# b_down added as a column on VectorE where it reads the transposed block from PSUM, zeros in DRAM in place of computed first sums, and the late modulation in f16 halves

## The reference, cut to what matters

```python
logits = h @ router_w + router_b
top_v, top_i = lax.top_k(logits, 4); gates = softmax(top_v)
gu  = xblk @ w_gu[e] + b_gu[e]                 # for the tokens of expert e
act = (clip(up) + 1.0) * gate * sigmoid(1.702 * gate)
yb  = act @ w_down[e] + b_down[e]
y   = sum over a token's four experts of yb * gate
x   = x + mod[:, 5] * rmsnorm(y, norm_g[3])
```

## Time and profile before

| | us |
|---|---|
| median of 3 runs | 2680.45 (2677.73 to 2681.34) |
| the profiled execution | 2680.32 |
| its span | 2678.6 |
| busy PE | 2439.7 (91%) |
| busy DVE | 1797.7 (67%) |
| busy ACT | 1553.6 (58%) |
| busy POOL | 799.2 (30%) |
| DMA | 536.90 MB, 200 GB/s over the span |

### The profile page before, as it was taken

One profiled execution on the slowest core, in us unless ns is written; L12 is line 12 of the kernel. 1 busy time (PEld: TensorE's weight loads), 2 busy tenths in 40 slices (PEclk: granted clock), 3 DMA queues, 4 the chain that ended last, 5 costly groups with the idle time before them and its releaser, 6 DMA issues. The chain is left out here.

```text
span 2678.6 us, 135745 instructions
## 1 busy us (share of the span) xinstructions
PE 2439.7 (91%) x57165; PEld 2162.2 (81%) x57165; DVE 1797.7 (67%) x2118; ACT 1553.6 (58%) x1964; POOL 799.2 (30%) x629
## 2 busy tenths in 40 slices
PE   6999998999989758999999999888998999999993
PEld 2555558999985448999898989888898999999993
DVE  3784986666657773361818386778777786789883
ACT  4523544555554442462827476777776676778773
POOL 3111105677740121221122222323222223232321
PEclk8899998999999968999999999999999999999996
DMA  8621001011023274381929496889888887899966
GB/s 286 248 76 56 1 1 49 25 31 31 23 70 101 95 291 138 119 308 29 356 73 331 125 370 225 305 312 376 320 304 310 311 299 256 281 337 359 344 238 207
DMA packets 123432, 536.90 MB, mean 200 GB/s; under 512 B 12237, under 2 KB 12609, under 8 KB 90561
## 3 DMA queue, kind: packets, MB, share of 16 engines
q1 hardware_dynamic: 107120, 481.80, 47.9%
q0 software_dynamic: 14880, 48.91, 8.2%
q10 hardware_dynamic: 1360, 5.24, 0.5%
HBM read 496.99 MB, written 38.92 MB: 200 GB/s over the span
## 5 line engine op out<-in xcount | busy, mean ns | idle before, releaser
L2499 PE MATMUL ps<-qkv,weights 128*128 128x64 f16 x10496 | 937.8, 193 | 65.9 <-DVE weights L1915 32.9
L2499 PEld LDWEIGHTS ps<-qkv,weights 128*128 128x128 f16 x10496 | 921.9, 98 | 82.4 <-issue 41.4
L2501 PE MATMUL ps<-qkv,weights 128*128 128x64 f16 x10496 | 937.4, 193 | 2.3 <-issue 2.3
L2500 PE MATMUL ps<-qkv,weights 128*128 128x64 f16 x10496 | 937.3, 193 | 0.5 <-issue 0.5
L2501 PEld LDWEIGHTS ps<-qkv,weights 128*128 128x128 f16 x10496 | 922.4, 98 | 0.6 <-issue 0.6
L2500 PEld LDWEIGHTS ps<-qkv,weights 128*128 128x128 f16 x10496 | 922.4, 98 | 0.0
L1915 DVE SCALAR_TENSOR_TENSOR weights<-hT,weights 128x2048 f16<-128x2048 f16 (+1 forms) x256 | 585.9, 2338 | 167.4 <-ACT weights L1299 137.4
L1299 ACT ACTIVATE weights<-hT 128x2048 f16 (+1 forms) x256 | 527.8, 2103 | 83.9 <-DMA hT<-in_w_gu_dram 67.0
L2516 PE MATMUL ps<-qkv,weights 128*128 128x64 f16 x5248 | 472.1, 193 | 23.4 <-DVE weights L1920 21.1
L2516 PEld LDWEIGHTS ps<-qkv,weights 128*128 128x128 f16 x5248 | 461.3, 98 | 30.8 <-DVE weights L1920 26.3
L2517 PE MATMUL ps<-qkv,weights 128*128 128x64 f16 x5248 | 471.8, 193 | 0.0
(11 more groups left out here) (446 smaller groups left out, 4305.0 us busy)
## 6 DMA issues: line engine op xcount, KB each, us to landing
hT<-in_w_gu_dram SPq DMA_DIRECT2D x256, 1024.0 KB, 9.1
qkv<-in_w_down_dram SPq DMA_DIRECT2D x128, 1024.0 KB, 6.1
weights<-in_w_ada_dram SPq DMA_DIRECT2D x8, 2048.0 KB, 14.1
qkv<-in_w_in_dram SPq DMA_DIRECT2D x4, 2048.0 KB, 9.2
qkv<-in_w_ada_dram SPq DMA_DIRECT2D x4, 2048.0 KB, 9.3
hT<-decay_rows SPq DMA_DIRECT2D x20, 256.0 KB, 3.3
hT<-beta_rows SPq DMA_DIRECT2D x20, 256.0 KB, 3.3
qkv<-in_x_dram ACTq DMA_DIRECT2D x4, 1024.0 KB, 8.1
```

Source lines behind the costliest of these rows:

```text
L2499: pe.matmul(dst, ghi[k][:, b, c], xT[:, 0, k, :], start=first, stop=False, skip_group_check=True)
L2500: pe.matmul(dst, ghi[k][:, b, c], xT[:, 1, k, :], start=False, stop=False, skip_group_check=True)
L2501: last = pe.matmul(dst, glo[k][:, b, c], xT[:, 0, k, :], start=False, stop=end, skip_group_check=True)
```

## The change: what it does

1. The first sums are gone: no `lgm`, `mixe3`, `y_start`, `copy_y_start`, `store_y_start`, nor the waits for them. b_down is loaded once rather than three times.
2. `y_scratch` is filled with zeros, by two DMAs of 2 MB on SP's queue during DeltaNet; the loads of decay and beta rows of the later chunks wait for them (`s_zero` 65 for 33).
3. PE turns b_down (32 x 1024) by eight transposes into columns, ACT copies them to `bdT`, 32 experts x 8 columns.
4. `copy_yT` goes from ACT to DVE. There it is one operation that reads PSUM, scales and adds the expert's eight columns, each repeated over 64 rows. It stands in DVE's iteration t behind `next_down(t+1)`.
5. Late modulation: DVE's sums get a factor (`csw` for `cs`), ACT makes f16 high halves of the eight sums (in the stage of the Z tiles), POOL the low halves, and PE sums each by two f16 matmuls against an f16 column of 1/WSCALE.

```diff
             for i in range(2):
+                sp.dma_start(y_d[i * SEQ // 2:(i + 1) * SEQ // 2, :].rearrange("(p r) d -> p (r d)", p=P),
+                             slot(5)).then_inc(s_zero, 16)
+            sp.wait_ge(s_zero, 65)
...
+            for q in range(FIRST, NADA):
+                pool.wait_ge(s_adar, q + 1)
+                high, low = (sum_halves[q - FIRST][:, j] for j in range(2))
+                pool.tensor_tensor(low, sums_of[q - FIRST], high, ALU.subtract).then_inc(s_colT, 1)
...
             gather(0)
-            for n in range(NT):
-                store_y_start(n)
             gather(1)
...
-            for i in range(2):
-                pool.wait_ge(s_yin[i], 16 * (5 - 2 * i))
...
+                for q in {0: range(FIRST, FIRST + 4), 3: (8,), 5: (9,), 6: (10,), 7: (11,)}.get(g - G_Z, ()):
+                    act.wait_ge(s_mod, q + 1)
...
+                    act.activation(sum_halves[q - FIRST][:, 0], sums_of[q - FIRST], ACT.Copy).then_inc(s_adar, 1)
...
-            def copy_yT(t):
-                act.wait_ge(s_dn, t * DK + 2 * DK)
-                reached(act, s_ty, t, 1, EMPTY)
-                act.activation(yT, ps[:, BT, :].rearrange("p (c t) -> p c t", c=8), ACT.Copy,
-                               scale=1.0 / (ALPHA * WSCALE * WSCALE)).then_inc(s_yT, 1)
...
                     high_act(t + 1)
-                    copy_yT(t)
                     scale_y(t - 1)
...
+            def copy_yT(t, e):
+                dve.wait_ge(s_dn, t * DK + 2 * DK)
+                reached(dve, s_ty, t, 1, EMPTY)
+                dve.scalar_tensor_tensor(yT, ps[:, BT, :].rearrange("p (c t) -> p c t", c=8), 1.0 / (ALPHA * WSCALE * WSCALE),
+                                         bdT[:, bass.ds(e * 8, 8)].unsqueeze(2).to_broadcast([P, 8, B]), ALU.mult,
+                                         ALU.add).then_inc(s_yT, 1)
...
                     next_down(t + 1, new1, r1)
+                    copy_yT(t, expert(t))
                     dve.sem_inc(s_idle, 1)
+            copy_yT(nlast, expert(nlast))
...
-                            last = pe.matmul(ps[:, 6, n:n + 1], sums_of[q - FIRST][:, a * P:(a + 1) * P], ones[:, 0:1],
-                                             start=True, stop=True)
+                            for j in range(2):
+                                last = pe.matmul(ps[:, 6, n:n + 1], sum_halves[q - FIRST][:, j, a * P:(a + 1) * P],
+                                                 ones16[:, 0:1], start=j == 0, stop=j == 1)
...
+            for k in range(KD):
+                last = pe.transpose(ps[:, 2, k * NE:(k + 1) * NE], bdn[:, k * P:(k + 1) * P], ident[0:NE, 0:NE])
+            last.then_inc(s_bdT, 1)
```

More of the change, by code:

```diff
@@ L148, in hybrid_block @@
         sums_of += [QK[:, 6 * D + 384 + 512 * i:6 * D + 896 + 512 * i] for i in range(1, 5)]
+        sum_halves = [QK[:, a:a + 512] for a in (14 * D, 14 * D + 512, 9 * D + 384, 5 * D + 384)] + sums_of[0:4]
+        sum_halves = [a.bitcast(F16).rearrange("p (j n) -> p j n", j=2) for a in sum_halves]
         tail = QK[:, 6 * D + 384:6 * D + 384 + 5 * 512]
@@ L157, in hybrid_block @@
         ident = sb("ident", [P, P])
-        ones = sb("ones", [P, P])
+        bdT = sb("ones_and_iota_then_b_down", [P, NE * KD])
+        ones, iota = bdT[:, 0:P], bdT[:, P:2 * P]
         tri = sb("tri", [P, DIRS, P])
@@ L251, in hybrid_block @@
         work = W[:, 12288:12288 + NT * TOPK * NE]
[L252 to L256, removed]
+        bdn = QK[0:NE, 14336:14336 + D]
         work = work.rearrange("p (n k e) -> p n k e", n=NT, k=TOPK)
@@ L617, in _ @@
                 load_rows(s, False)
-            sp.wait_ge(s_zero, 33)
+            for i in range(2):
+                sp.dma_start(y_d[i * SEQ // 2:(i + 1) * SEQ // 2, :].rearrange("(p r) d -> p (r d)", p=P),
+                             slot(5)).then_inc(s_zero, 16)
+            sp.wait_ge(s_zero, 65)
             with sp.Fori(NC, NA) as s:
@@ L625, in _ @@
             sp.dma_start(bgu_raw[0:NE, :], b_gu[0]).then_inc(s_bgu, 16)
-            for j in range(3):
-                sp.dma_start(bdn[j * NE:(j + 1) * NE, :], b_down[0]).then_inc(s_small, 16)
+            sp.dma_start(bdn, b_down[0]).then_inc(s_small, 16)
             sp.dma_start(rw, router_w[0].rearrange("(k p) e -> p k e", p=P)).then_inc(s_rw, 16)
@@ L1349, in scale_y @@
                                scale=gtab[:, bass.ds(t, 1)]).then_inc(s_yc, 1)
[L1351 to L1354, removed]
             def token_one_hots(q):
@@ L1366, in _ @@
             act.wait_ge(s_nb, 4)
[L1367 to L1374, removed]
+            for q in range(4):
+                token_one_hots(q)
+            act.wait_ge(s_bdT, 1)
+            act.activation(bdT[:].rearrange("p (e c) -> p c e", e=NE), ps[:, 2, 0:NE * KD].rearrange("p (c e) -> p c e", c=KD),
+                           ACT.Copy).then_inc(s_bdT, 1)
+            for k in range(4):
                 high_gate_up(0, 0, k)
-            copy_y_start(5)
-            high_gate_up(0, 0, 3)
-            copy_y_start(6)
             copy_xT(0)
             name_rows(1)
-            high_gate_up(0, 0, 4)
-            copy_y_start(7)
-            for k in range(5, GK):
+            for k in range(4, GK):
                 high_gate_up(0, 0, k)
-            for i in range(2):
-                act.wait_ge(s_yin[i], 16 * (5 - 2 * i))
             act.wait_ge(s_meta, 2)
-            act.sem_inc(s_yT, EMPTY)
             act.sem_inc(s_yc, EMPTY + 1)
@@ L1428, in _ @@
             scale_y(nprev)
-            copy_yT(nlast)
             scale_y(nlast)
@@ L1498, in weighted_rows @@
                 sums = sums_of[q - FIRST]
-                link(dve.tensor_scalar(sums, staged(q)[:, 0, :], cs[:, 0, 0:1], None, ALU.mult))
+                link(dve.tensor_scalar(sums, staged(q)[:, 0, :], csw[:, 0:1], None, ALU.mult))
                 for k in range(1, KD):
-                    link(dve.scalar_tensor_tensor(sums, staged(q)[:, k, :], cs[:, k, 0:1], sums, ALU.mult, ALU.add))
+                    link(dve.scalar_tensor_tensor(sums, staged(q)[:, k, :], csw[:, k:k + 1], sums, ALU.mult, ALU.add))
                 dve.sem_inc(s_mod, 1)
@@ L1991, in _ @@
             next_down(1, new, r)
+            copy_yT(0, expert(0))
             with dve.Fori(1, MAXB) as t:
@@ L2439, in _ @@
             pe.matmul(ps[0:1, 4, 256:256 + NB], endf[:], active, start=True, stop=True).then_inc(s_cnt, 1)
-            pe.wait_ge(s_mixe, 1)
+            pe.wait_ge(s_small, 146)
             pe.wait_ge(s_bgu, 19)
[L2443 to L2461, removed]
+            for k in range(KD):
+                last = pe.transpose(ps[:, 2, k * NE:(k + 1) * NE], bdn[:, k * P:(k + 1) * P], ident[0:NE, 0:NE])
+            last.then_inc(s_bdT, 1)
             M = NT * TOPK
             for m in range(M):
-                if m == 16:
-                    y_start(4)
                 if m % 8 == 0:
@@ L2527, in turn_y @@
                 last.then_inc(s_ty, 1)
-            pe.wait_ge(s_yev, 4)
+            pe.wait_ge(s_bdT, 2)
             turn_x(0)
-            y_start(6)
-            y_start(7)
             pe.sem_inc(s_dn, DK)
```

44 lines of the change are left out of this document (15 added, 29 removed).

## The result

The changed kernel takes 2718.69 us, median of 4 runs (2712.83 to 2724.20), beside 2679.09 for the kernel before (4 runs): ratio 1.0155, 95% interval 1.0132 to 1.0177. The forecast was 2714, slower. By the medians the change costs 39.6 us, where +34 was forecast. So some 7 us of the difference of the medians are in no trace.

What follows compares the result with a forecast made beforehand. PE (TensorE) was taken as the bound, other engines and DMA mattering only where PE waits. Terms -10.4 + 0 - 0.8 - 14 + 38 + 18 + 3 = +34 on 2680.3 gave 2714 us, range 2684 to 2730.

Steps and rivals of the forecast that it cites:

- part 1: Projections: 64 f16 passes replace 64 fp32 passes on PE and the clock holds; -10.4 us (-5.3 to -10.5).
- part 2: Zeros to y_scratch on SP's queue: written before the later row loads matter; 0 us (0 to +4).
- part 3: Output and router stage: small DVE operations and ACT copies go, most of them beside PE; -0.8 us (0 to -3).
- part 4: Start of expert loop: without the stores, DVE's idle time before L1915 and the gather wait go; -14 us (-9 to -20).
- part 5: Expert loop: copy_yT behind four low down chunks on DVE makes PE wait at nine places; +38 us (25 to 50).
- part 5b: Same nine places: PE's clock falls to half behind the waits, 2.0 us a place; +18 us (0 to +30).
- elsewhere in the loop: Other blocks: DVE has one more 0.69 us operation per block, mostly in its waits for PE; +3 us (-3 to +7).
- The mark that was set for the clock: Expert loop, nine places: granted clock shows half; a row staying full in the loop's first half would make the forecast wrong.
- rival D: Loop start doesn't give its 14 us and the clock falls in the modulation anyhow: 2727 us; chance 0.10.
- Rival B: Nine places in the loop: the waits come but the clock holds: 2696 us; chance 0.15.
- rival C: Nine places: the delay is given back, as PE's later waits shrink by the same amount: 2658 us; chance 0.15.

Runs made afterwards that it cites:

- the run with the increments: Changed kernel plus 31 one-instruction increments of an idle semaphore on PE ahead of the expert loop: 2713.28 us, ratio 1.0141 to the kernel before.
- the copy by case: Changed kernel, copy_yT ahead of the low down chunks where the block after next has a new expert, else behind the first: 2687.73 us, ratio 0.9975, slower chip.

## Why the prediction was right, and where two of its terms weren't

| term | forecast | trace after |
|---|---|---|
| part 1, modulation | -10.4 | -10.2 (first tile behind it 240.81 to 230.65; the passes began 0.24 later) |
| part 2, zeros | 0 | +0.2 (the shift is 10.2 at the start of DeltaNet, 10.0 at its end) |
| part 3, router stage | -0.8 | -1.0 |
| part 4, start of the loop | -14 | -7.9 |
| part 5, nine waits | +38 | +37.3 |
| part 5b, half clock | +18 | +16.1 |
| elsewhere in the loop | +3 | -2.0 |
| sum | +34 | +32.5 |

The three lines above the sum, in the last column, come from the ledger: before turn_y +68.2, in turn_y -2.7, in down -12.1, together +53.4. Of that 16.1 is the half clock (all that turn_y and down take over their undisturbed length in the kernel after, 7.0 and 9.1, as no chase of chunks is left in them), 37.3 the waits.

That the sum is within 2 us of the trace is in part luck: part 4 is 6.1 too high a gain, the rest of the loop 5.0 too high a cost, and they nearly cancel. The mark that was set for the clock, its row in the first half of the loop, was too coarse to be one: it shows 9 in every slice from 1017 to 2643 us, as before, while the clock fell nine times. Read as it was written it would have spoken against a forecast that was right. And rival D's 2727 doesn't follow from its terms: 14 + 5 above 2714 is 2733, and half of that 2724.

**Part 1** came out as worked out, with the clock held. The bound with the fall was not needed: 64 passes in 1.74 us are 27 ns each. The Trainium skill (TensorE: Matmul & The Clock Gate, LDWEIGHTS) gives, by its formula, 107 ns for a load of 128 columns; the profile's record of a load in the loop does last 98 ns, but loads overlap, so it is no measure of the time from one to the next, and the measured 27 decides.

**Part 5** is the step on which the result hangs, and the order on DVE gave it right: the wait of 8.41 us for 8.5, at nine places, released by the copy. The experiments show it by one instruction's place.

**Part 5b** rests on the row at 1005.70 and on part 1's rows. The trace after has one fall of the clock at each of the nine places, 6.8 or 10.2 us long, and in the run with PE kept busy down has its full speed at seven of them. Rival B is out. The Trainium skill (TensorE: Matmul & The Clock Gate, HAM oscillation) describes such a fall in each wait, and this trace agrees.

**Part 4 was mis-sized** by 6 us. The step that failed is "what they can win is DVE's idle time before L1915": DVE's waits there did shrink, from 7.4 to 3.2 us (2.15 and 1.08), but gate_up(0) is as long as before. It could have been seen: in the trace before no wait of PE from 984 to 1016 names L1915, so DVE's idle time didn't end in one of PE's. What makes gate_up(0) long in both traces is holes without a releaser (2.3 us before, 2.9 after) and the clock at half, after for the first 3 us and again behind the hole. What makes the holes stays open. The wait for the gather went as said, 5.5 us; with 1.1 between it and gate_up(1) (the hole is 0.8 shorter) and 1.3 from an earlier start of gate_up(0) the part gives 7.9. The mark set for it, gate_up(1) near 1001, doesn't fit the prediction's own sum, which puts it at 990 (1015.3 less 25); it began at 996.4.

**Not foreseen:** 12 us of gaps before gate_up, and 14 us less in gate_up. They cancel, and by the run with the increments that is no accident: take the one away and most of the other comes back. With the copy behind the first chunk it was about half (12.1 us taken away, the loop 6.6 shorter), over two chips. So rival C has a grain of truth. A delay of 0.2 us a block is given back in good part, one of 8.5 us in a single block isn't: of 68.2 us of new waits the nine places and the blocks behind them keep 50.8.

## What to carry to other kernels

When an operation is moved to an engine that runs in order, ask what stands ahead of it there and who waits for it; against the copy on the other engine the loop was 8, 22 or 48 us longer by the place of the same 0.7 us instruction among four of 2.3 us. Where an edit makes TensorE wait for long, look for a slow clock behind the wait: here waits of 8.4 us brought 16 us of it on top of 37. And a small saving that recurs in each pass of the loop is worth what the next waits leave of it, which only a run tells.

The kernel with the copy behind the first chunk and the increments, b_down added as in the change, is 0.46% under the kernel before (0.30 to 0.62%) where the change as made is 1.55% over.

## What the runs showed of the hardware

- PE's control code has a cost that depends on something outside the loop: the step from the first to the second instruction at its head took 0.095 us in seven kernels and 0.100 in the one with the 270 matmuls. In five it varied by block, with a median of 0.327 in four (the changed one and the three with the copy moved and no increments) and 0.214 in one (the copy by case). The cause is not settled, beyond that 4, 16 or 31 instructions put ahead of the loop remove it.
- A branch on PE over 270 matmuls that aren't executed cost 3.5 us in the block shown (branch at 1136.68, next instruction 1140.21). With the loop's body longer by them there was 3.9 us at the branch at the end of that block and 3.3 on the way back to its head, where the changed kernel has 0.3 and 0.1. This loop is 932 us longer than the changed kernel's, 11.65 us a block. The changed kernel's first pass through its loop has holes of 2.9 and 5.5 us with no releaser too; that the cause is the same is not shown.
- The copy with scale and column, from PSUM, took 0.684 us on DVE for 128 x 512 fp32, the same as the operation of its shape from SBUF (0.693).
